# Leaving out the 39 filler matmuls of each mixer

## The reference

```python
h = rms_norm(x, mix_norm[l])
pa, pb, pc, pd = jnp.split(h @ w_in[l], IN_SPLITS, axis=-1)
ya = neighbourhood_mixer(pa, ...)      # group A: local attention with a bias table
yb = mla_mixer(pb, ...)                # group B: latent attention, width 96 per head
yc = diff_mixer(pc, ...)               # group C: difference of two softmaxes
yd = gqa_mixer(pd, ...)                # group D: grouped-query attention
x = x + jnp.concatenate([ya, yb, yc, yd], axis=-1) @ w_out[l]
x = x + 0.5 * swiglu(rms_norm(x, ffn2_norm[l]), ffn2_w_gate[l], ffn2_w_up[l], ffn2_w_down[l])
```

## Time and profile before

| | |
|---|---|
| median of 3 runs | 1279.22 us (1278.36 to 1284.94) |
| the profiled execution | 1285.91 us, of which the span from the first to the last instruction 1283.6 us |
| TensorE, matmuls | 1251.2 us busy, 97% |
| VectorE | 847.1 us, 66% |
| ScalarE | 640.0 us, 50% |
| granted clock of TensorE, mean | 0.997 |

### The profile page before, as it was taken

The page is one execution under the profiler, slowest core; times in us unless marked ns, Lnnn a source line. Parts: engine busy times, 40 slices in busy tenths (PEclk is TensorE's granted clock), DMA queues, the critical chain, the costliest instruction groups (busy, mean ns, idle before and its releaser), DMA issues.

```text
span 1283.6 us, 24948 instructions
## 1 busy us (share of the span) xinstructions
PE 1251.2 (97%) x10578; PEld 1226.4 (96%) x10578; DVE 847.1 (66%) x1076; ACT 640.0 (50%) x857; POOL 79.6 (6%) x57
## 2 busy tenths in 40 slices
PE   7999999999999999999999999999999999999997
PEld 7999999989999999999999998999999999899996
DVE  6765666687766666876667687776666764446666
ACT  5333346766543334533335766543333554756543
POOL 1111011310000000000001121000000000000000
PEclk9999999999999999999999999999999999999999
DMA  8876565421466556466665532366555555325542
GB/s 287 242 222 197 178 230 164 153 100 39 160 212 189 191 196 195 161 211 197 196 202 170 154 130 67 99 204 193 195 196 196 187 182 178 118 82 158 172 150 113
DMA packets 171899, 220.34 MB, mean 172 GB/s; under 512 B 5360, under 2 KB 152560, under 8 KB 171696
## 3 DMA queue, kind: packets, MB, share of 16 engines
q1 hardware_dynamic: 168064, 213.66, 51.7%
q0 software_dynamic: 2080, 2.48, 1.1%
q10 hardware_dynamic: 1680, 3.13, 0.7%
HBM read 218.15 MB, written 3.42 MB: 173 GB/s over the span
## 4 chain that ended last, share of the span: by engine, by line
PE 86%; DVE 7%; ACT 5%; issue 1%; DMA 0%; SPq 0%; DVEq 0%; POOLq 0%; POOL 0%; ACTq 0%
PE pj L482 13%; PE pj L486 13%; PE pj L485 13%; PE acc L482 7%; PE acc L485 7%; PE acc L486 7%; PE tr L482 6%; PE tr L485 6%; PE tr L486 6%; PE acc L680 2%; PE acc L660 2%; ACT w_hi L955 1%; DVE w_lo L1272 1%; PE tr L650 1%; PE tr L672 1%
## 5 line engine op out<-in xcount | busy, mean ns | idle before, releaser
L1272 DVE TENSOR_TENSOR w_lo<-raw,w_hi 128x2048 fp32r<-128x2048 f32 (+1 forms) x205 | 456.4, 2227 | 231.0 <-ACT w_hi L955 229.6
L955 ACT ACTIVATE w_hi<-raw 128x2048 fp32r<-128x2048 f32 (+1 forms) x205 | 379.1, 1853 | 389.0 <-PE pj L482 141.5
L482 PE MATMUL pj<-hT_hi,w_hi 128*128 128x256 f32 x1056 | 295.7, 280 | 0.7 <-DVE scratch L1663 0.6
L486 PE MATMUL pj<-hT_hi,w_lo 128*128 128x256 f32 x1056 | 293.5, 278 | 0.0
L485 PE MATMUL pj<-hT_lo,w_hi 128*128 128x256 f32 x1056 | 293.5, 278 | 0.0
L482 PEld LDWEIGHTS pj<-hT_hi,w_hi 128*128 128x128 f32 x1056 | 198.5, 188 | 3.8 <-issue 2.4
L486 PEld LDWEIGHTS pj<-hT_hi,w_lo 128*128 128x128 f32 x1056 | 199.1, 189 | 0.0
L485 PEld LDWEIGHTS pj<-hT_lo,w_hi 128*128 128x128 f32 x1056 | 198.8, 188 | 0.3 <-issue 0.2
L482 PE MATMUL acc<-act_hi,w_hi 128*128 128x256 f32 x704 | 195.4, 278 | 2.9 <-issue 1.5
L485 PE MATMUL acc<-act_lo,w_hi 128*128 128x256 f32 x704 | 195.2, 277 | 0.0
L486 PE MATMUL acc<-act_hi,w_lo 128*128 128x256 f32 x704 | 195.2, 277 | 0.0
(11 more groups left out here) (219 smaller groups left out, 1874.0 us busy)
## 6 DMA issues: line engine op xcount, KB each, us to landing
raw<-in_w_in SPq DMA_DIRECT2D x47, 1024.0 KB, 5.3
raw<-in_ffn_w_down SPq DMA_DIRECT2D x44, 1024.0 KB, 5.0
raw<-in_ffn_w_gate SPq DMA_DIRECT2D x43, 1024.0 KB, 5.4
raw<-in_ffn_w_up SPq DMA_DIRECT2D x43, 1024.0 KB, 5.4
raw<-in_w_out SPq DMA_DIRECT2D x12, 1024.0 KB, 5.0
raw<-in_w_proj_a SPq DMA_DIRECT2D x4, 512.0 KB, 3.4
raw<-in_w_proj_b SPq DMA_DIRECT2D x4, 512.0 KB, 3.5
raw<-in_w_proj_c SPq DMA_DIRECT2D x4, 512.0 KB, 3.5
```

The costliest lines, as they stand in the source:

```text
L482: ins = pe.matmul(out, lhs[0], rhs[0], start=first, stop=False, **kw)
L486: return pe.matmul(out, lhs[1], rhs[0], start=False, stop=last, **kw)
L955: act.activation(w_hi[r % RING][:, 0:w], raw[r % RING][:, 0:w], ACT.Copy).then_inc(hi_set, 1)
L1272: dve.tensor_tensor(w_lo[r % RING][:, 0:w], raw[r % RING][:, 0:w], w_hi[r % RING][:, 0:w].bitcast(F32), ALU.subtract).then_inc(lo_set, 1)
```

## The change

The table is emptied, and with it 21 + 18 = 39 matmuls of each mixer go, 78 in all. Nothing else is different, and no step stands elsewhere.

```diff
-BUSY = {('pv', 4): 21, ('wout', 0): 18}
+BUSY = {}
```

## The result

The changed kernel is slower: 1298.31 us in the median (1295.22 to 1301.49, 4 runs) against 1282.08 (1278.36 to 1285.97, 4 runs), ratio 1.0117 with a 95% interval of 1.0086 to 1.0148. The forecast was 1281.3, within 1277.6 to 1286.5. Of the cases weighed it is the one called "the clock does not come back at once". Ratios leave out executions over 1.5% above the fastest of the same kernel; that concerns two of only21's ten alone (1300.13 and 1301.91 us).

A forecast was written before the change was run, and what follows sets the result against it. TensorE, busy 97% of the span, was taken as the bound. Fillers 0 - 0.7 us and two first clock falls +2.8 gave +2.1 us over the 1279.22 us median: 1281.3 us, range 1277.6 to 1286.5.

The forecast's parts named there:

- the clock does not come back at once: Rival: small matmuls after the first gap leave the clock low until the output projection; +9.0 us net per mixer; chance 0.12.
- Part 1: 21 fillers ahead of unit 4's weighting: L680 waits for ScalarE's copy anyway, so removing them gains 0.
- Part 2: 18 fillers ahead of the first output projection: of 2.2 us, 0.34 gained per mixer, since VectorE holds unit 7.
- Part 3: The clock: the new 3.0 us gap ahead of unit 4's weighting brings a fall in each mixer, 1.4 us each.
- The second fall: Another clock fall per mixer, between output projection and unit 7; even odds; with both, +4.9 us in all.
- The Trainium skill's rule on waits between bursts: Waits between matmul bursts put the array back to half rate; cited as speaking against removing the fillers; no size given.
- The Trainium skill's remark that the full rate doesn't engage for transposes: Full rate does not engage under transposes; cited as feeding the rival of the slow clock return; no size given.
- The sum: Both mixers together: fillers 0 - 0.7 us, two first falls +2.8 us, giving +2.1 us.

The follow-up runs named there:

- only21: Against the kernel before: the 18 fillers ahead of the output projection removed, the 21 ahead of unit 4's weighting kept; ratio 1.0032.
- placed8: Against the kernel before: the 18 fillers replaced by 8 between the transposes of units 6 and 7, 14 added at the third block's entry; ratio 1.0004.
- again: The changed kernel run once more on another occasion, with no edit; ratio to the kernel before 1.0097.
- late_turn: Against the kernel before: the 21 fillers removed, a burst of 30 128-column transposes put behind unit 4's weighting, the 18 kept; ratio 1.0081.
- fill_tail: Against the kernel before: 14 more dense fillers in the 1.81 us wait at the entry of the third block; ratio 0.9996.
- placed: Against the kernel before: the 18 fillers replaced by 12 between the transposes of units 6 and 7, 14 added at the third block's entry; ratio 1.0001.

## Why the prediction was wrong, point by point

- **Part 1, the 21 fillers cost nothing: right.** L680 starts 3.65 us after the interval's start with 21 fillers (284.80 - 281.15), with ten (285.14 - 281.49) and with none (284.99 - 281.34), in the last with a wait of 2.99 us for L1088.
- **Part 2, 0.34 us per mixer: right in mechanism, and 0.4 in size** (only21, placed8). That 2.2 us fewer at TensorE give 0.4 because unit 7 hangs on VectorE holds too.
- **Part 3, a fall at each of the first gaps: right. Its price: wrong.** This is the step that failed. I took 1.4 us from the one fall in the trace, and with it that the clock would be back after 3.4 us. (I read the edge of that fall 0.16 us late; the counts of 18 and 31 are the same with it put right.) That row is from a stretch of wide matmuls. Behind this gap stand weightings of 64 columns, transposes and scores of 32 rows, and the clock stayed down through them: 13.7 us, and 3.9 and 4.0 us of loss per mixer in the changed kernel's profile, where I had 1.4 less 0.34. I had this case, at 9 us per mixer and with a chance of 0.12. The size was over by a factor of two: I doubled all work from 284.8 to 293.5, but the scores took 2.61 us in place of 2.27 (296.53 - 293.92 against 292.65 - 290.38) and waits were absorbed. The chance was too small: rows 8, which I held against it, show the clock staying up under small matmuls, not returning. That the median, 1298.31, lies next to the 1297 of that case is luck: its 9 us per mixer were not there, and what makes up for them are things that the forecast did not have, the fall at the third block and the scatter from one execution to the next.
- **The second fall: even odds in the text, and left out of the number.** It came in both mixers in only21 and in again, and cost 2.9 and 3.2 us in only21, not 1.4. In the changed kernel's own profile it did not come. There the projection ran late, so the wait ahead of unit 6 was missing (1.08 us ahead of unit 7 alone, against 1.29 and 1.09 in again and 0.69 and 1.08 in only21), and the clock had come back only 2.2 us before; which of these kept it up is not shown.
- **The Trainium skill's rule on waits between bursts** (TensorE: Matmul & The Clock Gate, HAM oscillation) pointed the right way: behind L680's wait of 2.99 us the clock went to 0.50 at 285.8. The Trainium skill's remark that the full rate doesn't engage for transposes (the same page, Part 4) is not borne out: in late_turn the granted clock rose from 0.50 to 1.00 at 291.2, after 3.2 us of transposes.
- **The sum against what was measured.** Forecast +2.1 us; the two profiles of the changed kernel give 7.9 and 13.0 us in the mixers. The ratios, 1.0 to 1.2%, are 12 to 15 us. Between these lie the longer low stretch at the third block (1.6 us in one profile) and differences from one execution to the next: two of the changed kernel's four had a mean clock of 0.980 and 0.983 against 0.985 in the profile, and two feed-forward stages can each take 6 us more or less (last section), more together than my range of 9 us. How much each makes up is not shown.

## What to carry to other kernels

Fillers that end before the wait does cost nothing and can be worth more than they look: ask of each what the clock would do in the gap, and price a fall by the work that stands behind the gap, not by the nearest dense stretch. Behind a gap of 3 us the low level lasted from 3.4 to 13.7 us here, with the same narrow work behind it. Put fillers inside the wait, behind all work that is ready, and count them so that the last ends before the releaser does; a few too many cost as much as they save.

## What the hardware showed that I had not expected

A whole feed-forward stage runs at one of two speeds, by chance from one execution to the next. These are the same 60 us of the same instructions, at a granted clock of 1.00, in the profiles of before and of only21:

```profile
60.00:120.00 60.00, 60.00 (x511) 1.00 0.73 215
400.00:500.00 100.00, 100.00 (x885) 1.00 0.60 196
```

```profile
60.00:120.00 60.00, 60.00 (x532) 1.00 0.77 228
400.00:500.00 100.00, 100.00 (x885) 1.00 0.58 189
```

511 matmuls against 532, a pitch of 0.118 us against 0.113. Over the stage this made 6 us (the interval starts at 281.15 in before and at 275.03 in only21), and the times of fill_tail and of placed, whose clocks hardly fall, lie in groups near 1279, 1284.5 and 1292. I saw it in the first feed-forward part of either layer, never in the second, in kernels with and without the fillers. The profiles of before and of the changed kernel both had the slow pitch there, so the 9.3 us between them don't contain it. The clock is not its cause; what is stays open.
